# A bias added by VectorE in PSUM, moved into TensorE as a one-row product

## The reference, cut to what matters

```
def spatial_gating_mixer(u, v, w_s, b_s, ln_g, ln_b):
    u = gelu(u)
    v = layernorm(gelu(v), ln_g, ln_b)                 # (B, T/128, 128, 4, 128)
    w = where(tril, w_s, 0)                            # (4, 128, 128)
    sv = einsum('gts,bnsgc->bntgc', w, v) + transpose(b_s)[:, :, None]
    return u * sv
```

## Time and profile before

| | |
|---|---|
| median of 3 runs | 2188.36 us (2184.93 to 2196.56) |
| profiled execution | 2184.93 us |
| its span, first to last instruction | 2183.2 us |
| mean granted TensorE clock | 0.964 |
| TensorE matmul busy | 2027.1 us, 93% |
| VectorE busy | 1191.3 us, 55% |
| ScalarE busy | 936.8 us, 43% |

### The profile page before, as it was taken

The page is one execution under the profiler, slowest core; times in us unless marked ns, Lnnn a source line. Parts: engine busy times, 40 slices in busy tenths (PEclk is TensorE's granted clock), DMA queues, the critical chain, the costliest instruction groups (busy, mean ns, idle before and its releaser), DMA issues.

```text
span 2183.2 us, 27687 instructions
## 1 busy us (share of the span) xinstructions
PE 2027.1 (93%) x10514; PEld 1715.4 (79%) x10514; DVE 1191.3 (55%) x1417; ACT 936.8 (43%) x1189; POOL 216.6 (10%) x277
## 2 busy tenths in 40 slices
PE   6999999998999999997799899997899999999980
PEld 6988888887888888885699778886688888888860
DVE  4106642101433334240567667635888888888856
ACT  5123232211332333331235445312577777777742
POOL 0000000002020111000000000000122222222210
PEclk9999999999999999999899999997899999999995
DMA  4111224224232323212432175315799999999946
GB/s 172 41 59 58 77 87 154 89 106 142 84 119 97 129 101 138 100 52 88 171 107 100 49 265 179 139 78 188 274 369 377 381 388 385 384 386 381 378 166 240
DMA packets 125286, 397.35 MB, mean 182 GB/s; under 512 B 15039, under 2 KB 36047, under 8 KB 119263
## 3 DMA queue, kind: packets, MB, share of 16 engines
q1 hardware_dynamic: 107180, 352.07, 43.1%
q0 software_dynamic: 18016, 44.00, 5.7%
HBM read 343.39 MB, written 69.40 MB: 189 GB/s over the span
## 4 chain that ended last, share of the span: by engine, by line
PE 82%; issue 6%; DVE 6%; DMA 3%; ACT 2%; POOLq 0%; SPq 0%; POOL 0%; DVEq 0%; ACTq 0%
PE psum L605 22%; PE psum L607 22%; PE psum L606 22%; PE psum L2070 3%; PE psum L2200 2%; PE psum L2185 2%; PE psum L2418 1%; PE psum L2095 1%; DMA rows<-rows_scratch 1%; PE psum L2344 1%; PE psum L2037 1%; PE psum L2439 1%; PE psum L2083 1%; DVE yg L1961 0%; DVE x L1962 0%
## 5 line engine op out<-in xcount | busy, mean ns | idle before, releaser
L1876 DVE TENSOR_TENSOR e_l<-e_raw,e_h 128x2048 fp32r<-128x2048 f32 x190 | 424.5, 2286 | 36.6 <-ACT e_h L1216 36.0
L605 PE MATMUL psum<-hT_h,w_l 128*128 128x512 f32 x1088 | 434.0, 399 | 0.0
L607 PE MATMUL psum<-hT_h,w_h 128*128 128x512 f32 x1088 | 425.0, 391 | 0.0
L606 PE MATMUL psum<-hT_l,w_h 128*128 128x512 f32 x1088 | 424.5, 390 | 0.0
L1216 ACT CAST e_h<-e_raw 128x2048 fp32r<-128x2048 f32 x190 | 354.9, 1931 | 36.5 <-DMA e_raw<-in_w_e 20.0
L1324 DVE TENSOR_TENSOR w_l<-wraw,w_h 128x2048 fp32r<-128x2048 f32 (+1 forms) x38 | 87.0, 2289 | 286.9 <-ACT w_h L921 286.9
L607 PEld LDWEIGHTS psum<-hT_h,w_h 128*128 128x128 f32 x1088 | 204.6, 188 | 44.0
L605 PEld LDWEIGHTS psum<-hT_h,w_l 128*128 128x128 f32 x1088 | 204.9, 188 | 40.0
L606 PEld LDWEIGHTS psum<-hT_l,w_h 128*128 128x128 f32 x1088 | 205.1, 189 | 39.7
L605 PE MATMUL psum<-e_h,xT_l 128*128 128x512 f32 x512 | 203.0, 397 | 10.3 <-DVE xT_l L1882 10.2
L607 PE MATMUL psum<-e_h,xT_h 128*128 128x512 f32 x512 | 200.5, 392 | 0.0
(11 more groups left out here) (360 smaller groups left out, 3335.8 us busy)
## 6 DMA issues: line engine op xcount, KB each, us to landing
e_raw<-in_w_e SPq DMA_DIRECT2D x192, 1024.0 KB, 10.0
wraw<-in_w_in_t SPq DMA_DIRECT2D x37, 1024.0 KB, 4.8
pt_scratch<-stage SPq DMA_DIRECT2D x52, 512.0 KB, 2.6
gate<-pt_scratch SPq DMA_DIRECT2D x24, 512.0 KB, 3.8
rows<-rows_scratch SPq DMA_DIRECT2D x8, 1280.0 KB, 9.0
h_scratch<-xn SPq DMA_DIRECT2D x16, 512.0 KB, 3.6
yg<-expert_rows SPq DMA_DIRECT2D x8, 1024.0 KB, 13.4
conv_scratch<-co POOLq DMA_DIRECT2D x12, 512.0 KB, 2.9
```

Of the source, the lines that this page charges most:

```text
L605: nc.tensor.matmul(out_ap, ll, rh, start=first, stop=False)
L606: nc.tensor.matmul(out_ap, lh, rl, start=False, stop=False)
L607: return nc.tensor.matmul(out_ap, lh, rh, start=False, stop=last)
L1876: nv.tensor_tensor(e_l[:, c], e_raw[:, c], e_h[:, c].bitcast(F32), ALU.subtract).then_inc(s_el13 if c < 4 else s_el2, 1)
```

## The change

The bias becomes part of the product. `a_one` is a new tile with one row of 128 ones, and `a_bias` shrinks from 128 equal rows to one row. Behind each of the 32 products of mixer A's gate TensorE runs a second one into the same quarter of the bank, with one row of contraction: the ones as weights, the group's 128 biases as the streamed operand, accumulated onto the first. VectorE's eight additions (L1357) and the wait behind each go. GpSimd fills `a_one` at the start of the program, and the count that it and `bias_products` wait for becomes one higher. The transfer of `a_bias` shrinks from 256 KB to 2 KB.

```
-        a_bias = ra("a_bias", [P, NC])
+        a_one = ra("a_one", [1, P])
+        a_bias = ra("a_bias", [1, NC])
...
             pool.wait_ge(s_cst, 3)
+            pool.memset(a_one[:], 1.0).then_inc(s_amask, 1)
+            pool.wait_ge(s_amask, 1)
             pool.wait_ge(s_aload, 16 * 5)
             pool.memset(c_relb[REL_BUCKETS:REL_BUCKETS + 1, :], 1.0).then_inc(s_amask, 1)
-            pool.wait_ge(s_amask, 1)
+            pool.wait_ge(s_amask, 2)
...
                 dve.wait_ge(s_ev, groups_done(CH_B - 1))
-                sv, g = banks4(2 + n % 4), n % NH
-                bias = a_bias[:, g * HD:(g + 1) * HD].rearrange("p (a t) -> p a t", a=1)
-                cd.link(nv.tensor_tensor(sv, sv, bias.to_broadcast([P, 4, HD]), ALU.add))
                 nv.tensor_tensor(o, ps[2 + n % 4], o, ALU.mult).then_inc(s_ay, 1)
...
                 pe.wait_ge(s_aload, 16 * 5)
-                pe.wait_ge(s_amask, 2)
+                pe.wait_ge(s_amask, 3)
...
                     o = ps[2 + n % 4][:, a * P:(a + 1) * P]
-                    ins = mm(o, av[:, 4 * q + a, g * HD:(g + 1) * HD], aw[:, g], start=True, stop=True)
+                    mm(o, av[:, 4 * q + a, g * HD:(g + 1) * HD], aw[:, g], start=True, stop=False)
+                    ins = mm(o, a_one[:], a_bias[:, g * HD:(g + 1) * HD], start=False, stop=True)
                 ins.then_inc(s_asv, 1)
...
-        a_bs=lay(np.broadcast_to(a["a_b_s"][0].reshape(1, NC), (P, NC))),
+        a_bs=lay(a["a_b_s"][0].reshape(1, NC)),
```

## The result

The changed kernel takes 2226.61 us (median of 4 runs, 2225.44 to 2229.74) against 2190.6 us of the kernel before (4 runs, 2184.93 to 2196.56): 1.0161 times as long, interval 1.0139 to 1.0182, so about 36 us slower. The profiled execution took 2225.1 us with a span of 2223.4 us, 40.2 us more than the profiled one before, which was the fastest of its runs.

What follows compares the result with a forecast made beforehand. TensorE's own work was taken to bound the kernel from 63 to 1022 us. Columns 7.2, shape changes 11.5 and clock falls 6 made 24.7 us on 2184.93 us, so 2210 us, range 2193 to 2220 us.

Steps and rivals of the forecast that it cites:

- What bounds the kernel, and what goes: From 63 to 1022 us TensorE's own work sets the end; VectorE's 5.5 us and the smaller transfer are worth 0.
- Columns, 7.2 us: Gate's groups: 32 one-row products are 64 instructions at 0.112 us each, 7.2 us on the path.
- The doubt about the load: Gate's one-row products: whether a one-row weight load costs less than 128 rows; the sum would hardly change.
- Changes of shape, 64 x 0.18 = 11.5 us: Gate's groups: each change costs 0.09 us waiting and 0.09 us uncovered load; bounds 0 and 16.6 us.
- What is added by the clock: Slots 35, 37, 39 and 41: clock falls behind thin work, four times 1.5 us, 6 us; bounds 0 and 12 us.
- The stretch that lost the clock: Thin work in the trace before, where the clock fell after 3.96 us; slot 35's 4.9 us was likened to it.
- clock holds: Rival for the gate's slots: shape changes cost as worked out, clock stays 1.00; 18.7 us, 2203.6 us; chance 0.20.
- Columns only: Rival for the gate: shape changes are free; 7.2 us, 2192.1 us, up to 2195 us with falls; chance 0.18.
- half price: Rival for the gate: changes cost 0.09 us as the load hides; 13 us, 2197.9 us; chance 0.10.
- not slower: Whole kernel: the change does not make it slower; chance 0.05.

Runs made afterwards that it cites:

- the kernel with 128 rows: Changed kernel with both operands of the bias product filled to 128 rows, all but one row of ones zero: 2194.26 us, ratio 1.002 to the kernel before.
- the spread order: Changed kernel with each gate product, its one-row product and a quarter of the square sums behind a quarter of the slot's projection: 2214.11 us, ratio 1.0115 to before.

## Why the prediction was right and where it failed

It forecast slower, 2210 us with 2193 to 2220 us as the range. It is slower, but the measured 2226.61 us lies above the range. Point by point:

- **What bounds the kernel, and what goes:** right. TensorE is full in the stage and what is added there moves all behind it; VectorE's 5.5 us and the smaller transfer are worth 0 (stage +0.0 us without the addition).
- **Columns, 7.2 us:** right, 7.1 us in the kernel with 128 rows. The doubt about the load is settled: one row loads as long as 128 (0.29 and 0.30 us for two instructions).
- **Changes of shape, 64 x 0.18 = 11.5 us:** nearly right in size, 0.19 us each, 12.3 us, and the load starts with its own product at each change (210.38 and 210.38 us) as forecast. A group was to last 3.2 us; by the measure that gave 0.90 us before, it lasts 3.34 us. Not every other number of rows costs that: with 65 rows between neighbours of 128 the distance stays at 0.22 us, with 64 it is 0.31 and 0.42 us. What TensorE does at a change, and why 64 rows cost what 65 don't, no run shows.
- **"What is added by the clock", 4 falls x 1.5 us = 6 us:** this step failed. The stretch that lost the clock, with which it compares slot 35, is that of the earlier trace rows. That the clock can fall behind thin work with TensorE busy is right (three falls in the kernel before with its square sums doubled, 17.0 us at 0.50), though no run shows what in the work sets a fall off; but the term was two to three times too small: 17.6 us in the profiled execution and 12.8 us in the other, and even its upper bound, 12 us for eight falls of 3.41 us, was too low for both. Two assumptions in it were wrong. First, groups without square sums were taken to keep the clock; those of slots 34, 36 and 38 lost it as well. Second, every fall was given the 3.41 us of the earlier trace rows, which began when the 33-row products had all started; four of the seven began with square sums still to start, and lasted 6.80 us. The price per us was near right, 0.47 in place of 0.44 (1.5 / 3.41).
- **The rivals:** "clock holds" (18.7 us) describes the spread order, not this one. "Columns only" and "half price" fall by the spacings in slot 34, and "not slower", which was given 0.05, by the 0.73 us from one gate product to the next (210.07 to 210.80).

The 17.6 us are what the other two terms leave, so that they add up proves nothing. With the clock's price from the doubled square sums, 0.46 x 37.4 = 17.2 us, the sum is 7.2 + 12.3 + 17.2 = 36.7 us for the stage's 37.1 us. The bounds should have left the length open too: a fall seen once gives a price, not a length. The other 3.1 us of the profiled span come late: the last of the attention's products of L2070 is 36.8 us later than before (974.3 and 1011.1 us), and the end 40.2 us. No run looked at what is lost there, and the medians, 36 us apart, don't need it.

## What to carry to other kernels

Where TensorE is full, a product that moves work off an engine with time to spare is paid in full (here 7.1 us for 32 products of 128 rows), and with one row or 64 between neighbours of 128 it costs 0.19 to 0.20 us for each change besides. Give an extra product its neighbours' shape (zero-padded to 65 and to 128 rows it cost no changes here; in one trace of each the clock fell once and not at all), and pad a lone small product as well (its fall at 67.25 us was gone). One wide odd product in place of many narrow ones saves changes (16 in place of 64), but a long run of odd ones can lose the clock, as the 33-row products did in all 13 traces. Read the granted clock around every run of thin products, at full busy share too, and don't let two kinds of thin work stand back to back (with the square sums half a slot ahead of the gate the changed kernel had 6.8 us at half clock, against 37.4 and 27.2 us in two executions without that, a difference that can't be put down to the order alone).

## What the runs showed of the hardware that was not expected

- The granted clock fell from 1.00 to 0.50 seven times in one kernel with TensorE busy all the while, each time for 3.4 or 6.8 us, at 0.46 to 0.48 us lost per us. All 21 falls of 6.8 us up to 330 us, in fourteen traces, began with thin products still to start. Full-shape products of one column did it as well as one-row products.
- 64 rows and 65 rows with the same columns: +29.1 and +8.7 us for 32 products.
- Number and length of the falls differ between two executions of one kernel, seven and six (37.4 and 27.2 us at half clock), with 4.7 us between their stages.
